# Forgetting layer: keys, queries and probabilities turned on VectorE and carried between quadrants through DRAM, the value projection last

## The reference: what is computed

```
proj = h @ w_in                      # q, k, v (2048 columns each) and 32 forget logits
c = cumsum(log_sigmoid(f_logit + b_f))            # per head, over the 256 tokens
s = (q_i . k_j) * scale + c_i - c_j               # for j <= i, else -inf
out = softmax(s) @ v ;  y = out @ w_out
```

## Time and profile before

| | us |
|---|---|
| median of 3 runs | 2128.02 (2127.37 to 2129.18) |
| profiled execution, its own time | 2127.79 |
| its span, first to last instruction | 2125.9 |
| PE busy | 2113.3 |
| DVE / ACT / POOL busy | 1587.2 / 1179.3 / 120.9 |
| forgetting layer, from its first unit to its output projection | 997.6 to 1297.3 |

### The profile page before, as it was taken

The page is one execution under the profiler, slowest core; times in us unless marked ns, Lnnn a source line. Parts: engine busy times, 40 slices in busy tenths (PEclk is TensorE's granted clock), DMA queues, the critical chain, the costliest instruction groups (busy, mean ns, idle before and its releaser), DMA issues.

```text
span 2125.9 us, 32497 instructions
## 1 busy us (share of the span) xinstructions
PE 2113.3 (99%) x9791; PEld 1734.9 (82%) x9791; DVE 1587.2 (75%) x3256; ACT 1179.3 (55%) x2129; POOL 120.9 (6%) x231
## 2 busy tenths in 40 slices
PE   9999999999999999999999999999999999999998
PEld 7877888888888888888878877888888888888886
DVE  6777577877678876778787777577776678776686
ACT  7776565544555444555676566565454555445452
POOL 2111000000000000000231131000000000000000
PEclk9999999999999999999999999999999999999999
DMA  7644756555666655665665665666655665556652
GB/s 256 192 139 132 216 179 218 189 186 178 201 213 190 194 172 195 197 205 157 183 198 182 182 191 164 207 199 198 197 174 182 197 213 189 188 179 199 216 186 91
DMA packets 205549, 399.85 MB, mean 188 GB/s; under 512 B 13233, under 2 KB 13393, under 8 KB 204961
## 3 DMA queue, kind: packets, MB, share of 16 engines
q1 hardware_dynamic: 203008, 390.12, 58.8%
q0 software_dynamic: 2320, 8.72, 1.4%
q10 hardware_dynamic: 144, 0.07, 0.0%
HBM read 396.72 MB, written 2.13 MB: 188 GB/s over the span
## 4 chain that ended last, share of the span: by engine, by line
PE 98%; DVE 1%; issue 1%; DMA 0%; POOL 0%; ACT 0%; SPq 0%; POOLq 0%; DVEq 0%; ACTq 0%
PE bank L1193 31%; PE bank L1195 31%; PE bank L1194 31%; PE bank L1242 1%; PE bank L1269 1%; PE bank L1253 1%; PE bank L1206 1%; PE bank L1225 0%; DMA stage<-swa_w_in 0%; DVE ring_lo L732 0%; DVE x_sb L774 0%; DVE y_sb L993 0%; POOL post_r L1086 0%; DVE a_lo L739 0%; DVE y_sb L767 0%
## 5 line engine op out<-in xcount | busy, mean ns | idle before, releaser
L1193 PE MATMUL bank<-ring_hi,a_hi 128*128 128x512 f32 x2240 | 884.1, 395 | 1.5 <-DVE ring_lo L732 1.5
L1195 PE MATMUL bank<-ring_hi,a_lo 128*128 128x512 f32 x2240 | 873.2, 390 | 0.0
L1194 PE MATMUL bank<-ring_lo,a_hi 128*128 128x512 f32 x2240 | 872.1, 389 | 0.0
L539 ACT ACTIVATE ring_hi<-stage,g_t 128x512 fp32r<-128x512 f32 x992 | 663.3, 717 | 342.0 <-DMA stage<-ffn_w_gate_up 202.1
L732 DVE SCALAR_TENSOR_TENSOR ring_lo<-stage,g_t,ring_hi 128x512 fp32r<-128x512 f32 x992 | 706.6, 756 | 163.6 <-ACT ring_hi L539 162.0
L1193 PEld LDWEIGHTS bank<-ring_hi,a_hi 128*128 128x128 f32 x2240 | 420.6, 188 | 89.6 <-issue 4.1
L1195 PEld LDWEIGHTS bank<-ring_hi,a_lo 128*128 128x128 f32 x2240 | 420.4, 188 | 88.9
L1194 PEld LDWEIGHTS bank<-ring_lo,a_hi 128*128 128x128 f32 x2240 | 420.9, 188 | 83.3
L730 DVE TENSOR_TENSOR ring_lo<-stage,ring_hi 128x512 fp32r<-128x512 f32 x480 | 306.5, 688 | 131.7 <-ACT ring_hi L537 130.5
L537 ACT ACTIVATE ring_hi<-stage 128x512 fp32r<-128x512 f32 x480 | 277.3, 623 | 168.4 <-PE bank L1195 149.7
L1193 PE MATMUL bank<-ring_hi,h_hi 128*128 128x512 f32 x704 | 274.4, 390 | 0.0
(11 more groups left out here) (133 smaller groups left out, 850.5 us busy)
## 6 DMA issues: line engine op xcount, KB each, us to landing
stage<-ffn_w_gate_up SPq DMA_DIRECT2D x352, 512.0 KB, 4.6
stage<-ffn_w_down SPq DMA_DIRECT2D x176, 512.0 KB, 5.6
stage<-fox_w_in SPq DMA_DIRECT2D x96, 512.0 KB, 4.1
stage<-swa_w_in SPq DMA_DIRECT2D x48, 512.0 KB, 4.5
stage<-swa_w_out SPq DMA_DIRECT2D x64, 256.0 KB, 4.1
stage<-fox_w_out SPq DMA_DIRECT2D x32, 512.0 KB, 4.8
g_b<-norm_gains POOLq DMA_DIRECT2D x4, 1024.0 KB, 6.0
cum_b<-cum_scratch POOLq DMA_DIRECT2D x32, 128.0 KB, 3.5
```

The source lines that it names most:

```text
L539: nc.scalar.activation(ring_hi[:, n % RING, :], src, ACT.Identity, scale=g_t[:, row * KT + j:row * KT + j + 1]).then_inc(hi_ready, 1)
L1193: nc.tensor.matmul(dst, hi_a, hi_w, start=start, stop=False)
L1194: nc.tensor.matmul(dst, hi_a, lo_w, start=False, stop=False)
L1195: return nc.tensor.matmul(dst, lo_a, hi_w, start=False, stop=stop)
```

## The change

k and q units now come before v: k, q, v. The attention of a group starts in step 18 of its own v unit and is spread over 52 steps (table FOX): scores in steps 18 and 38, products with v in steps 50 and 70.

Nothing of the layer is turned on PE any more. DVE turns k with one instruction (128 partitions x 1024), q with one for each t (128x512), and each pair of heads' probabilities with two (128x256 and 128x512). These turn each 32x32 block in place, inside its own quadrant. POOL then stores the tile to a DRAM scratch and loads it back with four DMAs, one for each quadrant, which puts each block in the quadrant that it belongs to: k 512 KB, q 256 KB for each t, a pair of probabilities 384 KB. POOL's program is written out for the four groups, with the bias work between the stores and the loads. PE waits for `k_loaded` and `q_loaded` before a group's first scores, and for `p_loaded` before each pair's product with v. For the scores the stationary operand is now read from `q_f` with a step of four elements (16 bytes); keys and probabilities are read in runs of 32 elements.

```diff
+FOX = dict(scores={18: (0, 1), 38: (2, 3)},
+           maxima={18: (0, 1), 24: (2, 3), 38: (4, 5), 44: (6, 7)},
+           exps={19: 0, 20: 1, 25: 2, 26: 3, 39: 4, 40: 5, 45: 6, 46: 7},
+           scaled={23: 0, 29: 1, 43: 2, 49: 3}, turned={},
+           pv={50: (0, 1), 70: (2, 3)}, out={51: 0, 71: 1})
+FOX_LAST = dict(FOX, out={})
...
-KEYS_TURNED = {True: (26, 27, 28, 30), False: (3, 7, 11, 15)}
-QUERIES_TURNED = (18, 20)
+KEYS_TURNED = (1, 4)
+QUERIES_TURNED = {(1, 18): 0, (2, 2): 1}
...
+        k_f = at("k_f", 24 * KB, [P, P // Q, NT, GH // 2, Q])
+        q_f = at("q_f", 28 * KB, [P, NT, P // Q, Q, GH // 2])
+        p_f = at("p_f", 38 * KB + 256, [P, 2, P // Q, 6, Q])
+        k_blocks = at("k_blocks", 28 * KB, [P, P // Q, NT * (GH // 2) * Q])
+        q_blocks = at("q_blocks", 48 * KB + 256, [P, P // Q, (GH // 2) * Q])
+        p_blocks = at("p_blocks", 12 * KB, [P, P // Q, 6 * Q])
...
+        k_dram = nc.dram_tensor("k_scratch", (P, GH // 2 * SEQ), F32, kind="Internal").ap()
+        q_dram = [nc.dram_tensor(f"q_scratch{t}", (P, GH // 2 * P), F32, kind="Internal").ap() for t in range(NT)]
+        p_dram = [nc.dram_tensor(f"p_scratch{m}", (P, 6 * P), F32, kind="Internal").ap() for m in range(HP)]
...
-                return cols(fox_w_in[0], c * CH + (D, 2 * D, 0)[part] + i * CH)
+                return cols(fox_w_in[0], c * CH + (D, 0, 2 * D)[part] + i * CH)
...
+            eng.wait_ge(qk_turned, 3 * c + (t - 1 if part == 0 else 1) + 3 * i)
...
+            if U_FOX <= u < U_FOX_OUT and (u - U_FOX) % 3 == 2:
+                return NG + (u - U_FOX) // 3
...
+            for v, at_step in ((u - 2, s + 2 * STEPS), (u - 1, s + STEPS), (u, s)):
...
+            def turn_keys(u, i):
+                dve.wait_ge(proj_read, 2 * mixer_unit(u) + 2 + 6 * i)
+                src = stg[:, :, :].rearrange("p t (k b j) -> p (t k) b j", b=P // Q, j=Q)
+                dst = k_blocks[:, :, :].rearrange("p b (n i) -> p n b i", i=Q)
+                nc.vector.transpose(dst, src).then_inc(qk_turned, 1)
+            def turn_queries(u, i, t):
+                dve.wait_ge(proj_read, 2 * mixer_unit(u) + t + 1 + 6 * i)
+                before = 2 * ((u - U_FOX) // 3) + t
+                if before:
+                    dve.wait_ge(q_stored, 16 * before + 32 * i)
+                src = stg[:, t, :].rearrange("p (k b j) -> p k b j", b=P // Q, j=Q)
+                dst = q_blocks[:, :, :].rearrange("p b (i k) -> p k b i", i=Q)
+                nc.vector.transpose(dst, src).then_inc(qk_turned, 1)
+            def turn_probabilities(G, i, m):
+                n = HP * (G - NG) + m
+                dve.wait_ge(normed, GH * G + 2 * m + 2 + GH * i)
+                if n > 0:
+                    dve.wait_ge(p_stored, 16 * n + 16 * HP * i)
+                pair = prob[:, 2 * m % 4:2 * m % 4 + 2, :]
+                nc.vector.transpose(p_blocks[:, :, 0:2 * Q].rearrange("p b (h i) -> p h b i", i=Q),
+                                    pair[:, :, columns(0)].rearrange("p h (b j) -> p h b j", j=Q))
+                nc.vector.transpose(p_blocks[:, :, 2 * Q:6 * Q].rearrange("p b (h t i) -> p h t b i", t=2, i=Q),
+                                    pair[:, :, columns(1)].rearrange("p h (t b j) -> p h t b j", t=2, j=Q)).then_inc(p_turned, 1)
...
+                            if (part, s) == KEYS_TURNED:
+                                turn_keys(u - 1, i)
+                            if (part, s) in QUERIES_TURNED:
+                                t = QUERIES_TURNED[part, s]
+                                turn_queries(u - t, i, t)
...
+                            if G >= NG:
+                                turn_probabilities(G, i, when["scaled"][at_step])
...
+            def load_blocks(dst, dram, loaded):
+                blocks = dram.rearrange("(a j) (b r) -> b j a r", a=P // Q, b=P // Q)
+                for b in range(P // Q):
+                    pool.dma_start(dst[Q * b:Q * (b + 1)], blocks[b]).then_inc(loaded, 16)
+            def store_keys(c):
+                pool.wait_ge(qk_turned, 3 * c + 1)
+                pool.dma_start(k_dram, k_blocks[:, :, :].rearrange("p b r -> p (b r)")).then_inc(k_stored, 16)
+            def load_keys(c):
+                pool.wait_ge(k_stored, 16 * (c + 1))
+                load_blocks(k_f[:, :, :, :, :].rearrange("p a t k i -> p a (t k i)"), k_dram, k_loaded)
+            def store_queries(c, t):
+                pool.wait_ge(qk_turned, 3 * c + t + 2)
+                pool.dma_start(q_dram[t], q_blocks[:, :, :].rearrange("p b r -> p (b r)")).then_inc(q_stored, 16)
+            def load_queries(c, t):
+                pool.wait_ge(q_stored, 16 * (2 * c + t + 1))
+                load_blocks(q_f[:, t, :, :, :].rearrange("p a i k -> p a (i k)"), q_dram[t], q_loaded[t])
+            def store_probabilities(c, m):
+                pool.wait_ge(p_turned, HP * c + m + 1)
+                pool.dma_start(p_dram[m], p_blocks[:, :, :].rearrange("p b r -> p (b r)")).then_inc(p_stored, 16)
+            def load_probabilities(c, m):
+                pool.wait_ge(p_stored, 16 * (HP * c + m + 1))
+                pool.wait_ge(pv_done, 2 * (NG + c) + m // 2)
+                load_blocks(p_f[:, m % 2, :, :, :].rearrange("p a n i -> p a (n i)"), p_dram[m], p_loaded[m % 2])
...
+                if n < 4:
+                    pool.wait_ge(pt_done, GH * NG)
+                else:
+                    pool.wait_ge(p_turned, (n - 4) // 2 + 1)
...
+                if n + 4 < GH * NG:
+                    pool.wait_ge(biased, n + 1)
+                    load_cum((n + 4) // GH, (n + 4) % GH)
...
+                    for c in range(NG):
+                        store_keys(c)
+                        load_keys(c)
+                        if c > 0:
+                            for j in range(4):
+                                bias(c, j)
+                        store_queries(c, 0)
+                        load_queries(c, 0)
+                        if c == 0:
+                            pool.wait_ge(cum_made, 1)
+                            pool.dma_start(cum_dram, cum_t[:, :]).then_inc(cum_stored, 16)
+                            pool.wait_ge(cum_stored, 16)
+                            for j in range(4):
+                                load_cum(0, j)
+                        store_queries(c, 1)
+                        if c == 0:
+                            bias(0, 0)
+                            bias(0, 1)
+                        load_queries(c, 1)
+                        if c == 0:
+                            bias(0, 2)
+                            bias(0, 3)
+                        for m in range(HP):
+                            store_probabilities(c, m)
+                            if m < 2:
+                                bias(c, 4 + 2 * m)
+                                bias(c, 5 + 2 * m)
+                            load_probabilities(c, m)
...
+                elif m == 0:
+                    pe.wait_ge(k_loaded, 64 * (G - NG + 1) + 64 * i)
+                    for t in range(NT):
+                        pe.wait_ge(q_loaded[t], 64 * (G - NG + 1) + 64 * i)
...
+                        else:
+                            q, k = q_f[rows, t, :, :, m].rearrange("p a i -> p (a i)"), k_f[rows, :, 0:t + 1, m, :].rearrange("p a t i -> p t a i")
+                        last = nc.tensor.matmul(score_bank(G, 2 * m + a)[:, lo:lo + keys], q, k, start=True, stop=True)
...
+                        elif part == 0 and a == 0:
+                            pe.wait_ge(p_loaded[m % 2], 64 * (2 * (G - NG) + m // 2 + 1) + 128 * i)
...
+                        elif part == 0:
+                            p = p_f[:, m % 2, :, a:3 + 2 * a:2 + a, :].rearrange("p a t i -> p t a i")
+                        else:
+                            p = p_f[:, m % 2, :, 3 + 2 * a, :]
+                        last = nc.tensor.matmul(dst, v_sb[:, part, v0:v0 + DH], p, start=part == 0, stop=part == 1)
```

More of the change, by code:

```diff
@@ L130, in transposes_in_order @@
             use("qk", u, 0)
-    for c in range(NG):
-        use("qk", U_FOX + 3 * c + 2, 1)
     return number
 TR = transposes_in_order()
-TR_LOOP = TR[("qk", U_FOX + 8, 1)] - TR[("qk", U_FOX + 5, 1)]
 def build(nc, x, positions, norm_gains, swa_w_in, swa_sinks, swa_w_out,
@@ L405, in holds_qk @@
         def holds_qk(u):
-            return u in (0, 2, 3, 4, 5) or (U_FOX <= u < U_FOX_OUT and (u - U_FOX) % 3 != 1)
+            return u in (0, 2, 3, 4, 5)
         def qk_transposed(u, s):
@@ L425, in is_v @@
         def is_v(u):
-            return u == 1 or (U_FOX <= u < U_FOX_OUT and (u - U_FOX) % 3 == 1)
+            return u == 1 or (U_FOX <= u < U_FOX_OUT and (u - U_FOX) % 3 == 2)
         def out_chunk(u):
@@ L795, in turn_queries @@
-            def turn_queries(u, i, half):
-                if half == 0:
-                    dve.wait_ge(proj_read, 2 * mixer_unit(u) + 1 + 6 * i)
-                for a in (2 * half, 2 * half + 1):
-                    for b in range(P // Q):
```

(38 more changed lines are left out.)

67 lines of the change are left out of this document (22 added, 45 removed).

## The result

| | before | after |
|---|---|---|
| median, us | 2128.16 (2127.37 to 2129.18, 4 runs) | 2155.06 (2153.22 to 2160.19, 4 runs) |
| profiled execution / span, us | 2127.8 / 2125.9 | 2153.2 / 2151.1 |
| ratio | | 1.0132, 95% interval 1.0119 to 1.0145 |

The account below looks back on a forecast made before the run. PE was taken to bound the kernel, busy for 2113.3 of 2125.9 us. From 2127.8, less 13.2 for removed work, plus 11.2 of waits for probabilities and 7.0 for queries, gave 2132.8 us; range 2115 to 2147.

Parts of the forecast that it names:

- The direction: Whole kernel: slower, 2132.8 us against 2127.8; chance of slower 0.49, of faster 0.33.
- The removed part: PE in the forgetting layer: the transposes leave it, taking off 13.2 us.
- I count both at nothing: DVE and ACT in the layer: neither bounds a unit, so their changed work was priced at zero.
- The trip: DRAM store and four loads in front of PE: 10.6 us from turned to loaded, store landing 3.9, loads 3.5.
- the congestion rival: The layer's DMA: landings of 5 us and more throughout, time 2140 to 2155 us; chance 0.16.
- Probabilities: PE before the products with v: waits of 2.8 us a group, 11.2 us for four.
- Queries: PE before a group's first scores: waits of 2.5 us in group 0 and 1.5 in each other, 7.0 in all.
- The 16-byte step: Scores' weight loads from q_f: possibly slower, left out of the sum; chance 0.12 of over 3 us on top.
- its lower case: Scores' weight loads at twice the time: four short slots of each of 8 events grow, 3.3 us, 2136 in all.
- The landings by the Trainium skill: DMA trips at 2.0 us plus bytes over 436 GB/s: some 2.3 us shorter, time near 2120; not used in the sum.

Follow-up runs that it names:

- run 2: The changed kernel with all operands of scores and products with v read in rows from x_sb and no timely waits for loads (values wrong): 2115.74 us, ratio 0.9940.
- Run 8: The changed kernel with each weight load of the layer's q, k and v units bringing only half its columns: 2137.32 us, ratio 1.0039.
- Run 3: The changed kernel with ten 128x128 identity matmuls on PE ahead of its wait for q_f and k_f: 2154.13 us, ratio 1.0119.
- run 7: The changed kernel with a second buffer for the turned queries and both query stores ahead of the first loads: 2149.59 us, ratio 1.0096.
- runs 1: The changed kernel with operands read from x_sb with the same steps and no timely waits for loads (values wrong): 2120.06 us, ratio 0.9961.
- run 10: The kernel before with eight longer pauses of PE (2.79 to 7.43 us idle) in both feed-forward layers: 2186.73 us.

## Why the prediction was wrong

The direction was right, and so was its kind: PE waits for the two trips, and the sign hangs on it. Two steps of the working failed and one was missing: the landings of the trip were taken too short, the price of the 16-byte step was put at nothing, and the lower clock behind a wait was no term. One by one:

- *The removed part* holds: -13.2 in the sum; run 2, with operands in rows and no wait for a load, ran 12.8 us under the kernel before (2115.74 against 2128.58). "I count both at nothing" for DVE and ACT holds in the change (no wait of PE in the attention ends at either), though q's turn took 1.11 us where I had 0.70. The first unit behind the attention took 21.76 us, as before (1376.34 to 1398.10).
- *The trip.* "A store of 256 to 512 KB lies between: 3.9 to 4.5", loads 3.5. They measured 5.1 (P) and 5.3 (q) for the stores, 4.4 for the loads of P. With the trips, the DMA share is 0.91 in a unit where it was 0.66. I knew this as the congestion rival and gave it 0.16, and took the middle of before's landings, whose traffic was another. Run 8 and the spread of P's stores show the cause.
- *Probabilities:* 11.2 us forecast, 12.1 measured. That is luck. I had 2.8 us in every group; the first three waited for 1.7 to 2.5 and the last for 6.2, half of the whole. The trips were longer than I had them, but the scores came 2 to 4 us late, and PE's step with them. Run 3 fits that, with earlier scores and 1.2 us more of waits for P, but doesn't prove it.
- *Queries:* 7.0 forecast, 12.3 measured. The order of POOL and the 20.5 us to the first store (20.9 forecast) were right, and "the second store starts then" too. The two landings one behind the other were what failed: in group 2 the first store took 6.9 us and the second 5.0, where I had 3.9 each, and the last load landed 40.2 us into the q unit instead of at 38.3. A second buffer and both stores ahead of the loads take 6.7 us of waits away (run 7).
- *The 16-byte step:* "I leave it out of the sum." It costs 5.3 us in the trace and 4.3 between runs 1 and 2, more than the 3.3 of its lower case, which counted four short slots an event; there are eight of 128 keys and eight of 256 (64 and 64 matmuls in eight events). The Trainium skill, Advanced Engine Details and Errata, section SBUF Cachelines, says that a different line at each access costs, and the runs agree (324 against 187 ns). My hope that it would be absorbed was wrong. For the moving operand in runs of 32 elements nothing was lost.
- *The lower clock* stood nowhere: 9.1 us. I priced a wait at its length, and no row of before shows more, since PE never waited there for more than 0.75 us.
- *The landings by the Trainium skill.* The Trainium skill, DMA: Bandwidth & Descriptors, section Anatomy of one DMA, would have put a store of 384 KB at some 2.9 us, as an estimate. That is what the five stores beside hardly any weight loads took, 2.6 to 3.2; the median with the weight loads was 5.1, and 3.4 with half of them. The measurement decides: the figure is that of a quiet queue, and these trips don't run in one.

Of the 20.6 us by which the profiled sum was missed (25.6 against 5.0), 9.1 are the clock, 5.3 the step, 6.2 the waits. The longer waits and the step were small chances of their own, which the range treated as alternatives, and the clock was none. They add up, and a longer wait brings the clock with it.

## What to carry to other kernels

A trip through DRAM in front of a saturated engine is worth what its last landing leaves of slack, priced with the traffic that it will meet and not with the quiet landings of before. Count all trips in one queue as a chain: a later step for the consumer delays the next trip if a buffer is freed by it. A wait of over 2 us nearly always cost PE more than its length here, about 1.7 us for each spell of 3.4 us, and some of 1.3 to 1.9 us did too, so halving a wait isn't shown to save it. Take the part of such a change whose operands stay in rows and whose deadline is far, and leave the rest.

## What the runs showed of the hardware

- PE's weight load depends on the step of the stationary operand (324 against 187 ns at 128 fp32 columns, 16 bytes apart), its matmul not on runs of 32 in the moving one.
- DVE's transpose of 128x512 took 1.10 to 1.13 us with a destination step of 16 bytes (q) and 0.67 in runs of 32 elements (P).
- A store of 384 KB landed in 2.6 to 3.2 us beside hardly any weight loads and in 4.5 to 7.2 beside them, its median moving from 5.1 to 3.4 with half the weight traffic.
- Idle time of PE alone brings a spell at 0.50 (run 10): one of 3.4 or 6.8 us at each pause of 3.2 us and more, none at 0.3 to 1.8 and at 2.79 us. In the layer, waits from 1.3 us on brought some and every wait of 2.04 us and more did.
